# Output projections with split fp32r weights, and both operand parts in one 512-column matmul at 256 tokens

## What is computed

```python
# first block, both layers
merged = g[:, :, 0] * o_a + g[:, :, 1] * o_b + g[:, :, 2] * o_c
return merged @ w_out
...
# second block, layer 0: tokens and context
out = jnp.concatenate([fourier_mix(a), chunk_sgu(u, v, g_v, w_s, b_s)], axis=-1)
return out @ w_out
...
# second block, layer 1: tokens only
out_x = blocked_attention(q_x, k_all, v_all) @ w_o[j]
...
# the feed-forward parts: 2 in the first block, 4 in the second
return (jax.nn.silu(a) * b) @ w_down
return x + 0.5 * gate * swiglu(modulated_norm(x, g, shift, scale), w_gu, w_down)
```

## Time and profile before

| | |
|---|---|
| median of 3 runs | 2864.05 us (2862.58 to 2865.24) |
| the profiled execution | a span of 2864.8 us, 0.75 us above the median |
| TensorE matmul | 2791.6 us busy, 97% of the span, 15884 instructions |
| TensorE weight load | 2309.3 us, 81% |
| DVE, ACT, POOL | 58%, 38%, 6% |
| DMA | 446 MB, 156 GB/s over the span |

### The profile page before, as it was taken

The page is one execution under the profiler, slowest core; times in us unless marked ns, Lnnn a source line. Parts: engine busy times, 40 slices in busy tenths (PEclk is TensorE's granted clock), DMA queues, the critical chain, the costliest instruction groups (busy, mean ns, idle before and its releaser), DMA issues.

```text
span 2864.8 us, 38787 instructions
## 1 busy us (share of the span) xinstructions
PE 2791.6 (97%) x15884; PEld 2309.3 (81%) x15884; DVE 1666.9 (58%) x2355; ACT 1098.5 (38%) x1660; POOL 170.0 (6%) x132
## 2 busy tenths in 40 slices
PE   7999999999999999999999999999999999999998
PEld 5778888987778889877878766888877788878998
DVE  4798447646985477645456435554564545363554
ACT  3545336544553366422222323222232222234443
POOL 0070000000620000000000000000000000000000
PEclk9999999999999999999999999999999999999999
DMA  8642457656523576455454212443335543221453
GB/s 328 203 155 78 142 179 237 222 169 217 173 71 127 191 242 221 146 183 191 147 191 155 81 57 82 147 148 132 140 118 186 185 145 138 96 96 50 165 183 112
DMA packets 122464, 446.23 MB, mean 156 GB/s; under 512 B 13488, under 2 KB 14896, under 8 KB 121904
## 3 DMA queue, kind: packets, MB, share of 16 engines
q1 hardware_dynamic: 122288, 443.76, 45.2%
HBM read 442.66 MB, written 1.05 MB: 155 GB/s over the span
## 4 chain that ended last, share of the span: by engine, by line
PE 89%; DVE 6%; ACT 3%; DMA 1%; issue 1%; SPq 0%; DVEq 0%; ACTq 0%
PE ps L613 23%; PE ps L615 23%; PE ps L614 23%; PE ps L617 20%; DVE area L1752 1%; DVE rests L1649 1%; DVE rs L1712 1%; DMA ring<-stream 1%; ACT L1310 0%; ACT L1493 0%; DVE area L1722 0%; ACT work L1310 0%; DVE rs L1912 0%; ACT L1264 0%; ACT heads L1250 0%
## 5 line engine op out<-in xcount | busy, mean ns | idle before, releaser
L613 PE MATMUL ps<-h_split,heads 128*128 128x256 f32 (+1 forms) x2992 | 992.5, 332 | 15.2 <-DVE h_split L1730 7.6
L614 PE MATMUL ps<-h_split,heads 128*128 128x256 f32 (+1 forms) x2992 | 970.0, 324 | 0.0
L615 PE MATMUL ps<-h_split,rests 128*128 128x256 f32 (+1 forms) x2992 | 969.7, 324 | 0.0
L1649 DVE TENSOR_TENSOR rests<-ring,heads 128x1024 fp32r<-128x1024 f32 x520 | 648.3, 1265 | 292.7 <-ACT heads L1250 285.1
L1250 ACT ACTIVATE heads<-ring 128x1024 fp32r<-128x1024 f32 x520 | 536.5, 1056 | 521.9 <-PE ps L615 299.8
L613 PEld LDWEIGHTS ps<-h_split,heads 128*128 128x128 f32 x2992 | 571.7, 191 | 120.3 <-ACT rt L1350 23.5
L614 PEld LDWEIGHTS ps<-h_split,heads 128*128 128x128 f32 x2992 | 571.9, 191 | 48.8 <-issue 5.3
L615 PEld LDWEIGHTS ps<-h_split,rests 128*128 128x128 f32 x2992 | 571.6, 191 | 45.2
L613 PE MATMUL ps<-hid_split,heads 128*128 128x256 f32 (+1 forms) x1056 | 355.1, 336 | 0.0
L615 PE MATMUL ps<-hid_split,rests 128*128 128x256 f32 (+1 forms) x1056 | 354.9, 336 | 0.0
L614 PE MATMUL ps<-hid_split,heads 128*128 128x256 f32 (+1 forms) x1056 | 354.8, 336 | 0.0
(11 more groups left out here) (184 smaller groups left out, 2482.7 us busy)
## 6 DMA issues: line engine op xcount, KB each, us to landing
ring<-stream SPq DMA_DIRECT2D x834, 512.0 KB, 3.5
consts<-constants SPq DMA_DIRECT2D x1, 1728.0 KB, 11.1
x_sb<-x_in SPq DMA_DIRECT2D x1, 1024.0 KB, 12.0
x_sb<-ctx_in SPq DMA_DIRECT2D x1, 1024.0 KB, 4.7
out<-area SPq DMA_DIRECT2D x1, 1024.0 KB, 4.8
consts<-constants SPq DMA_DIRECT2D x1, 576.0 KB, 8.8
cols<-columns SPq DMA_DIRECT2D x1, 538.0 KB, 9.9
cols<-columns SPq DMA_DIRECT2D x1, 157.5 KB, 2.3
```

Of the source, the lines that this page charges most:

```text
L613: nc.tensor.matmul(out, lhsT[0], rhs[0], start=first, stop=False)
L614: nc.tensor.matmul(out, lhsT[0], rhs[1], start=False, stop=False)
L615: ins = nc.tensor.matmul(out, lhsT[1], rhs[0], start=False, stop=last)
L1649: nc.vector.tensor_tensor(rests[:, u % RING, :], ring[:, u % RING, :], as_f32(heads[:, n % HEADS_RING, :]), ALU.subtract)\
```

## The change

1. `is_split` now names `oa_` and `ob_`, and no longer `out` and `o2`: the blocks of `out_0`, `out_1`, `oab` and `o2` are split. These are 4 x 64 blocks, 32 units.
2. Their operands are split: ACT writes heads into `hr[:, 0]`, DVE writes rests into `hr[:, 1]`. For `out_l` heads and rests are made from `merged`, a step behind the merge of the next m. For `oab`, k = 0 to 3 are made from the banks of the Fourier part, k = 4 to 7 from `mixed`. For `o2` both are made from the attention's output bank.
3. Where the width is 256 and rhs has three members, `product` issues two matmuls in place of three: heads of the weights by a moving operand of 2 x 256 columns (heads and rests of the activation side by side) into 512 columns of a bank, and rests of the weights by heads into the first 256. This holds for `out_0`, `out_1`, `o2` and the three down projections at 256 tokens. `oab` has the three matmuls of 512 columns.
4. `update` then reads both halves of the bank: an instruction more for each m, and the second one waits for the first, since both add to the same x.

```diff
-    return name is not None and not name.startswith(("mod", "uq", "uk", "uv", "pw2", "oa", "ob", "out", "o2"))
+    return name is not None and not name.startswith(("mod", "uq", "uk", "uv", "pw2", "oa_", "ob_"))
...
+        def hid_both(j):
+
+            return hidr[:, :].rearrange("p (w c) -> p w c", w=2)[:, :, j * SEQ:(j + 1) * SEQ]
...
-                if isinstance(lhsT, tuple):
+                if isinstance(lhsT, tuple) and len(rhs) == 3:
+                    nc.tensor.matmul(out, lhsT[0], rhs[2], start=first, stop=False)
+                    ins = nc.tensor.matmul(out[:, 0:SEQ], lhsT[1], rhs[0], start=False, stop=last)
+                elif isinstance(lhsT, tuple):
...
+            def three_of(k, t):
+
+                return hr[:, 0, k, t], hr[:, 1, k, t], hr[:, :, k, t]
...
-                linear_pair([take_bank((p, "out", m))[:, 0:SEQ] for m in range(2)], f"out_{l}", late(range(KD)), 0,
-                            lambda k: merged[:, k, :], [(p, "out", m) for m in range(2)],
-                            once(lambda k: pe.wait_ge(vector_done, V.at((p, "merged", k)))))
+                both = lambda k: three_of(k, slice(SEQ, TOK))
+                linear_pair([take_bank((p, "out", m)) for m in range(2)], f"out_{l}", late(range(KD)), 0,
+                            both, [(p, "out", m) for m in range(2)],
+                            once(lambda k: pe.wait_ge(vector_done, V.at((p, "mergedr", k)))))
...
+                def merged_heads(m):
+                    act.wait_ge(vector_done, after(V, (p, "merged", m)))
+                    nc.scalar.activation(hr[:, 0, m, SEQ:TOK], merged[:, m, :], ACT.Copy)\
+                      .then_inc(scalar_done, A.mark((p, "mergedh", m)))
...
                     for g in range(4):
-                        copy_pair(mixed[:, g, :], (p, "f", g))
+                        act.wait_ge(tensor_done, after(T, (p, "f", g)))
+                        nc.scalar.activation(hr[:, 0, g, :], bank((p, "f", g)), ACT.Copy)\
+                          .then_inc(scalar_done, A.mark((p, "mixedh", g)))
+                    for g in range(4):
+                        act.wait_ge(vector_done, after(V, (p, "sgu", g)))
+                        nc.scalar.activation(hr[:, 0, 4 + g, :], mixed[:, 4 + g, :], ACT.Copy)\
+                          .then_inc(scalar_done, A.mark((p, "mixedh", 4 + g)))
...
-            def update(p, what, T_, gate):
+            def update(p, what, T_, gate, apart=False):
...
                     dve.wait_ge(tensor_done, after(T, (p, *what, m)))
+                    if apart:
+                        step(nc.vector.scalar_tensor_tensor(out=x[:, 0, m, :], in0=bank((p, *what, m))[:, SEQ:TOK],
+                                                            scalar=gate(m, 0), in1=x[:, 0, m, :],
+                                                            op0=ALU.mult, op1=ALU.add))
...
+                def merged_rests(m):
+                    dve.wait_ge(scalar_done, after(A, (p, "mergedh", m)))
+                    nc.vector.tensor_tensor(hr[:, 1, m, SEQ:TOK], merged[:, m, :], as_f32(hr[:, 0, m, SEQ:TOK]),
+                                            ALU.subtract).then_inc(vector_done, V.mark((p, "mergedr", m)))
...
+                    def output_rests(c):
+                        dve.wait_ge(scalar_done, after(A, ((p, "at"), "oh", c)))
+                        nc.vector.tensor_tensor(hr[:, 1, c, 0:SEQ], bank(((p, "at"), "o", c))[:, 0:SEQ],
+                                                as_f32(hr[:, 0, c, 0:SEQ]), ALU.subtract)\
+                          .then_inc(vector_done, V.mark(("read", ((p, "at"), "o", c))))
```

More of the change, by code:

```diff
@@ L1081, in _ @@
                     linear_pair([take_bank((p, "out", m)) for m in range(2)], "oab", late(range(KD)), 0,
[L1082 to L1084 removed]
+                                hx, [(p, "out", m) for m in range(2)],
+                                once(lambda k: pe.wait_ge(vector_done, V.at((p, "mixedr", k)))))
                     for m in range(2, KD):
[L1086 removed]
+                        linear(take_bank((p, "out", m)), "oab", KD, m, hx, (p, "out", m))
                 else:
@@ L1776, in head_norm, with attention @@
                         between(c - 1)
-            def attention(p, tasks, J, minus, between=None):
+            def attention(p, tasks, J, minus, between=None, last=lambda t: None):
                 def first(t):
@@ L2040, in _, with gated_rests @@
                     for g in range(4):
+                        dve.wait_ge(scalar_done, after(A, (p, "mixedh", g)))
+                        nc.vector.tensor_tensor(hr[:, 1, g, :], bank((p, "f", g)), as_f32(hr[:, 0, g, :]),
+                                                ALU.subtract).then_inc(vector_done, V.mark((p, "mixedr", g)))
+                        V.found[("read", (p, "f", g))] = V.found[(p, "mixedr", g)]
+                    def gated_rests(g):
+                        dve.wait_ge(scalar_done, after(A, (p, "mixedh", 4 + g)))
+                        nc.vector.tensor_tensor(hr[:, 1, 4 + g, :], mixed[:, 4 + g, :], as_f32(hr[:, 0, 4 + g, :]),
+                                                ALU.subtract).then_inc(vector_done, V.mark((p, "mixedr", 4 + g)))
+                    for g in range(4):
                         dve.wait_ge(tensor_done, after(T, (p, "mx", g)))
@@ L2067, in _ @@
                     key_rope(1)
-                    attention((p, "at"), 16, 1, lambda t: rs[:, 32 + t:33 + t])
+                    def output_rests(c):
[3 more added lines that the diff above has]
+                          .then_inc(vector_done, V.mark(("read", ((p, "at"), "o", c))))
+                    attention((p, "at"), 16, 1, lambda t: rs[:, 32 + t:33 + t],
+                              last=lambda t: output_rests((t - 3) // 2) if t >= 4 and t % 2 == 0 else None)
+                    output_rests(KD - 1)
                 T_ = TOK if l == 0 else SEQ
-                update(p, ("out",), T_, gate(5))
+                update(p, ("out",), T_, gate(5), T_ == SEQ)
                 adapted(2)
```

42 lines of the change are left out of this document (26 added, 16 removed).

## The result

The changed kernel takes **2846.95 us**, the median of four runs (2845.79 to 2849.23), against 2863.32 of the kernel before on the same chip (2861.41 to 2865.24): ratio 0.9943, interval 0.9930 to 0.9957. A later comparison gave 2847.20 against 2863.62, ratio 0.9949 (0.9936 to 0.9963). It is faster, as forecast, but by 16.4 us and not by 30.3, outside the range of 2828 to 2843.

The account below looks back on a forecast made before the run. TensorE was taken to bound the changed stages. Savings of 16.3 (output projections), 11.4 (oab) and 7.0 (down projections), 34.7 us, less 2.4 + 1.0 + 0.5 + 0.5 coming back, leave 30.3: 2834 us, range 2828 to 2843.

Parts of the forecast that it names:

- copies and subtractions of weights: 32 more units on ACT (1.056 us) and DVE (1.265), costed at nothing, hidden by matmuls; DVE margin 0.5 us a unit.
- Rival 2: Output projections: first weight units reach TensorE late through ACT and DVE, 9.3 us in all, 2843 us; chance 0.07.
- the pair: Two matmuls a block at 256 tokens, output and down projections: 0.3467 us, summed from parts 0.2267 and 0.1200.
- Both ends: Bounds on a pair's time: 0.3200 us with nothing fixed left, 0.5492 if the operand in two pieces streams badly.
- The forecast's own spread: Whole kernel: 2830 us with all of what comes back hidden, 2844 with the pair no better than three matmuls.
- fp32 and triples: Block prices: fp32 0.4317 us (256), 0.8584 (512); three split matmuls 0.3600, 0.6801; oab 11.4 less, waiting about 0.5.
- The norm behind an output projection: Behind out_0, out_1, o2: fourth copy ahead of the last two squares costs 0.79 us each, 2.4 in all.
- Oab's 0.96: Norm behind oab, 512 columns: 0.96 us later, from 4.63 behind f1down_0 against 3.67 behind oab.
- The second half of the bank: Second update instruction: 0.52 us for each m, hidden except at the final norm, which has no weights behind it.
- Rival 1: Weight load sets the pace at 256 columns; joining removes one of three: 19.2 us together, 2815 us; chance 0.04.
- Rival 3: Operand in two pieces streams badly: each of 720 pairs up to 0.2025 us more, 2980 us; chance 0.03.
- Joining: Two matmuls made one saves only the fixed part, 0.0133 us; 7.0 us over 528 down-projection blocks.

Follow-up runs that it names:

- experiment 1: Changed kernel with ACT's weight copies behind an output projection made one unit ahead, before its wait for the update: 2834.58 us, ratio 0.9904.
- experiment 2: Changed kernel with DVE's subtractions of weights put behind the updates in output projections: 2834.75 us, ratio 0.9901.
- experiment 6: Changed kernel with three matmuls a block and one update in the three output projections at 256: 2839.56 us, ratio 0.9921.
- experiment 10: Experiment 1 with the fourth copy behind the root and its subtraction on DVE behind the norm: 2837.51 us, ratio 0.9911.
- experiment 4: Changed kernel with heads and rests of the hidden values side by side in the down projections at 256: 2847.14 us, ratio 0.9945.
- the two grouped kernels: Matmuls of the pairs grouped by length, on top of experiment 1 (2834.58 us) and on top of experiment 2 (2835.52 us).
- experiment 7: Changed kernel with three matmuls a block and one update in the three down projections at 256: 2851.63 us, ratio 0.9961.
- experiment 9: The changed kernel itself, run once more on another comparison's chip: 2847.20 us.

## Why the prediction was wrong

**The step that failed** is the cost of *copies and subtractions of weights*: "I cost it at nothing; what hides it is the matmuls, with a margin of 0.5 us a unit on DVE." The work of each engine was counted well: DVE has 1.14 + 2 x 0.5 us for an output (2.3 in the forecast), ACT 1.04 + 0.42. But each was compared with TensorE's 2.77 by itself. The two wait for each other once in each direction at every output, so that they work in turn, and the time of an output is the sum round the cycle, 3.57. Experiments 1 and 2 cut the cycle and the lateness went; experiment 6 made it shorter and the lateness went too. Rival 2 had the wrong condition for the same reason ("once DVE needs over 2.77 us a unit"), and looked for the delay as a wait of TensorE at the start. It came at the end, as a late norm, 3.8 + 3.8 + 3.9 = 11.5 us. The norm behind down_0, which I took as the model, has the same orders, but an output takes TensorE 22 x 0.353 = 7.8 us there, and its gap is 2.64 before and after.

**The term that was mis-sized** is the pair: 0.3533 for 0.3467. That is 3.5 us in the down projections and 1.3 in the output projections (0.6, 0.6 and 0.1, with the longer first step of out_0 and out_1 among them). Both ends, 0.3200 and 0.5492, were far off; the sum of the parts was a little too good for this order of matmuls. Why this order costs more stays open.

Together 11.5 + 3.5 + 1.3 = 16.3; 30.3 - 16.3 = 14.0 us, and 0.1 better in oab. The trace from out_0 on has 15.4. The rest is the net of differences in the stretches between, which weren't followed: 1.7 us less in the one ahead of o2, 0.8 less in the one from 2133 to 2452 us of the kernel before, 1.3 more between down_0 and out_1. The forecast's own spread reached 2844, which its range of 2828 to 2843 already left out.

Point by point:

- **fp32 and triples**: right. Oab takes 43.92 for 43.5 + 0.5. Its wait is some 0.2 us and not 0.5 (from 1684.89 to 1685.23 and on to 1685.57, 0.34 us each, where a matmul has 0.227).
- **The norm behind an output projection**, 0.79 more: right once the cycle is cut. The reciprocal comes 3.75 us behind the matmuls of ones in experiment 1, 3.7 by the forecast, 6.41 in the changed kernel. Oab's 0.96 is 0.95 (3.71 - 2.76).
- **The second half of the bank**: 0.5 at the final norm as forecast, and hidden by the copy elsewhere (experiment 10: without the copy 2.25, which is 1.72 + 0.53). That "all but the last m is hidden" is wrong by experiment 6.
- **Rival 1**, the weight load as the pace: it did not come. In down_0 the loads' busy share fell from 48.00 of 48 us to 43.40 of 50:

```profile
550.00:600.00 50.00, 50.00 (x285) 43.40 (x284) 29.16 (x33) 22.25 (x26) 3.71 (x5) 1.00 0.54 185
```

  and a block got 2% faster, not a tenth. A weight load that is busy all the time was no bound here. The argument that the prediction had against this rival, that two kinds of matmul lie on one line, was none, since two points always do; it is the run that decides. The page Perfetto Trace Analysis of the Trainium skill, section Identifying the Most-Contended Engine, has the busy share of weight loads, beside the share of the peak arithmetic, as the measure of TensorE's headroom; a share of 100% as a bound is a reading with which this run disagrees.
- **Rival 3**, the operand in two pieces: excluded by experiment 4 in the down projections; and no pair anywhere comes near its 0.5492.
- **Joining** is worth 6.7 ns a block (13.4 only in the three rows of the last section). That is half the 13.3 that the rows gave and over twice the 2.5 of the formula on the page TensorE: Matmul & The Clock Gate of the Trainium skill, section Back-to-back issue gap; neither was right for this order of lengths. The page gives that formula for an isolated matmul and says that it is off in a row, where the prediction used it.

## What to carry to other kernels

When work is added to two engines that hand things to each other, don't compare each one's busy time with the bounding engine's pace: walk round the cycle of waits in the order of issue, add it up, and compare that with the pace. Here the lag brought no wait on the bounding engine while the stage lasted; it showed in the chain of waits as a repeated pattern, and was paid where the stage ended. It is cut where one engine can make its share one step earlier, as three lines did here for 12 us.

## What was not expected of the hardware

The same row of pairs has two paces. The traces with the change, those of the two grouped kernels left aside, have 51 long rows of alternating pairs. In 48 of them a pair takes 353.2 to 353.4 ns, with the distances 236, 113, 233, 117, 241, 120 in turn. In the other 3 it takes 346.6: o2 of the changed kernel and of experiments 7 and 10. The first of them:

```profile
2618.02 0.28 PE L618 MATMUL ps<-h_split,rests 128*128 128x256 f32 x1
2618.14 0.39 PE L617 MATMUL ps<-h_split,heads 128*128 128x512 f32 x1
2618.37 0.27 PE L618 MATMUL ps<-h_split,rests 128*128 128x256 f32 x1
2618.48 0.40 PE L617 MATMUL ps<-h_split,heads 128*128 128x512 f32 x1
2618.71 0.28 PE L618 MATMUL ps<-h_split,rests 128*128 128x256 f32 x1
```

The second run of the same program (experiment 9) has 353.4 there. The three rows at 346.6 have 312 or 313 ns between their first two matmuls, the five o2 rows at 353.2 to 353.4 have 314 to 318; after that each keeps its pace to the end. 346.6 is the forecast's sum of the parts. What sets a row's pace was not tried, and eight rows are few to tie it to the first distance.
